# Turning the latent-attention key projection over: one key per partition, then transposed, with ten weight splits moved from GpSimd to VectorE

## The reference, cut to what matters

```python
def mla_expand(c_kv, k_rope, w_kvup, qk_k_norm):
    B, K = c_kv.shape[0], c_kv.shape[1]
    kv = (c_kv @ w_kvup).reshape(B, K, MLA_HEADS, MLA_NOPE_DIM + MLA_V_DIM)
    k_nope, v = kv[..., :MLA_NOPE_DIM], kv[..., MLA_NOPE_DIM:]
    kr = jnp.broadcast_to(k_rope[:, :, None, :], (B, K, MLA_HEADS, MLA_ROPE_DIM))
    k = rmsnorm(jnp.concatenate([k_nope, kr], axis=-1), qk_k_norm)
    return k, v
```

## Time and profile before

| | us |
|---|---|
| median of 3 runs | 1162.91 |
| lowest, highest | 1159.22, 1162.91 |
| profiled execution, its own time | 1165.85 |
| profiled execution, span from first to last instruction | 1164.0 |
| TensorE busy | 1124.8 (97%) |
| VectorE, ScalarE, GpSimd busy | 642.1, 508.1, 353.4 |
| mean granted TensorE clock | 0.976 of full |

### The profile page before, as it was taken

How to read it: one execution, slowest core, us unless ns; L and a number is a source line. 1 busy time by engine, 2 the same in 40 slices (tenths; PEclk the granted TensorE clock), 3 DMA queues, 4 the chain that set the end, 5 groups by cost and what they waited for, 6 DMA issues and landing times.

```text
span 1164.0 us, 21685 instructions
## 1 busy us (share of the span) xinstructions
PE 1124.8 (97%) x7726; PEld 1076.0 (92%) x7726; DVE 642.1 (55%) x1018; ACT 508.1 (44%) x874; POOL 353.4 (30%) x242
## 2 busy tenths in 40 slices
PE   5899999999999999999989999999999999999998
PEld 4798889899999999999978988998999999999998
DVE  5635665444566655653355457654445756665443
ACT  4453534544454444433244434545444544444322
POOL 3566325465112111100027653455531211111000
PEclk9998879999999999999989988999999999999999
DMA  6422222332443544444433232233235444444443
GB/s 207 149 87 98 96 73 91 109 109 93 145 161 114 177 144 152 154 146 153 154 101 110 85 103 91 92 109 100 101 109 163 146 132 165 154 144 146 162 145 118
DMA packets 46823, 148.04 MB, mean 127 GB/s; under 512 B 8185, under 2 KB 11353, under 8 KB 46745
## 3 DMA queue, kind: packets, MB, share of 16 engines
q1 hardware_dynamic: 40472, 144.07, 37.2%
q10 hardware_dynamic: 6272, 2.92, 0.9%
HBM read 143.75 MB, written 3.22 MB: 126 GB/s over the span
## 4 chain that ended last, share of the span: by engine, by line
PE 86%; DVE 5%; issue 4%; DMA 2%; POOL 2%; ACT 1%; SPq 0%; ACTq 0%; DVEq 0%; POOLq 0%
PE psum L407 25%; PE psum L408 24%; PE psum L409 24%; POOL wsum L1567 1%; DMA scratch<-brel 1%; PE psum L466 1%; PE psum L513 1%; PE psum L506 1%; DVE tR L1368 1%; PE psum L518 1%; DVE stdk L1149 1%; PE psum L488 1%; PE psum L651 1%; PE psum L653 1%; PE psum L652 1%
## 5 line engine op out<-in xcount | busy, mean ns | idle before, releaser
L407 PE MATMUL psum<-AH,WH 128*128 128x320 f32 x1344 | 428.6, 319 | 14.2 <-DVE AL L1137 14.2
L408 PE MATMUL psum<-AL,WH 128*128 128x320 f32 x1344 | 419.9, 312 | 0.0
L409 PE MATMUL psum<-AH,WL 128*128 128x320 f32 x1344 | 419.7, 312 | 0.0
L407 PEld LDWEIGHTS psum<-AH,WH 128*128 128x128 f32 x1344 | 256.5, 191 | 27.4 <-DVE AL L1137 18.1
L1523 POOL TENSOR_TENSOR WL<-raw,WH 128x1024 fp32r<-128x1024 f32 x86 | 209.4, 2444 | 231.2 <-ACT WH L805 230.2
L805 ACT CAST WH<-raw 128x1024 fp32r<-128x1024 f32 x178 | 185.2, 1044 | 185.2 <-PE psum L409 169.9
L408 PEld LDWEIGHTS psum<-AL,WH 128*128 128x128 f32 x1344 | 257.0, 191 | 0.8 <-issue 0.2
L409 PEld LDWEIGHTS psum<-AH,WL 128*128 128x128 f32 x1344 | 256.7, 191 | 0.0
L1123 DVE TENSOR_TENSOR WL<-raw,WH 128x1024 fp32r<-128x1024 f32 x90 | 110.0, 1224 | 132.6 <-ACT WH L805 131.7
L1275 DVE TENSOR_TENSOR WL<-raw,WH 128x1024 fp32r<-128x1024 f32 x88 | 107.6, 1223 | 49.3 <-ACT WH L914 48.2
L1528 POOL TENSOR_TENSOR fab<-fa,fb 128x320 f32<-128x320 f32 x44 | 38.7, 880 | 269.6 <-DVE fb L1280 269.6
(11 more groups left out here) (230 smaller groups left out, 1691.7 us busy)
## 6 DMA issues: line engine op xcount, KB each, us to landing
raw<-w_all SPq DMA_DIRECT2D x267, 512.0 KB, 3.3
X<-x_in SPq DMA_DIRECT2D x2, 640.0 KB, 5.1
y_out<-X SPq DMA_DIRECT2D x2, 640.0 KB, 4.1
ckv<-lat_in ACTq DMA_DIRECT2D x2, 512.0 KB, 5.1
lat_out<-ckv ACTq DMA_DIRECT2D x2, 320.0 KB, 2.9
scratch<-brel SPq DMA_DIRECT2D x1, 510.0 KB
cst<-cst_in SPq DMA_DIRECT2D x1, 481.0 KB, 8.8
bias<-scratch SPq DMA_DIRECT2D x8, 48.0 KB, 2.2
```

What stands on the lines that cost most here:

```text
L407: mm(out, WH[:, slot, c0:c0 + cols], high, start=first, stop=False)
L408: mm(out, WH[:, slot, c0:c0 + cols], low, start=False, stop=False)
L409: return mm(out, WL[:, slot, c0:c0 + cols], high, start=False, stop=last)
```

## The change

The K projection is turned over and done like that of V, in seven blocks of 128 keys (`key_rows`): latents stationary, 512 key columns (8 heads by 64) moving, result with one key per partition. The norm is then a sum along the free axis: ScalarE squares (`key_square`), VectorE sums (`tensor_reduce`), ScalarE takes the root of eight numbers a key (`key_root`), VectorE takes the reciprocal and scales the plain columns into `Kn` (`key_scale`), GpSimd scales the rotary columns. TensorE transposes each head back (`turn_keys`, eight transposes a block), and ScalarE and VectorE copy four heads each into `Kt`, with the gain (`key_columns`). The rotary rows are turned once a layer (`turn_rope`). `stat_k`, `turn_k`, `spread_k`, `apply_k`, `square_k` and GpSimd's copies of the rotary rows are gone. The last `turn_keys` stands behind the first of the ten units.

VectorE splits units 12 to 21 (those for which q runs, `U_POOL + q + 1 + LEAD`), which GpSimd did before; GpSimd still splits unit 11, and VectorE waits for that at q = 0. GpSimd clears `qz` later, after that split, since `Kn` and `sqn` share its memory. ScalarE's rounding of unit 7 moves ahead of `ckvH`; units 7 to 9 are split by GpSimd one after the other. The product of the two gains is made inside the layer and no longer before the loop.

```diff
+        def key_rows(l, kb):
+
+            if kb == 0:
+                pe.wait_ge(s.tile_free, l * NT + T_QL + 2)
+            elif kb >= 2:
+                pe.wait_ge(s.kn_ready, l * KB + kb - 1)
+            out = psum[:, kbank(kb), :]
+            for c in range(2):
+                kh, kl = ckvH[:, c, key0(kb):key0(kb) + 128], ckvL[:, c, key0(kb):key0(kb) + 128]
+                wh = WH[:, U_KVK % RING, :].rearrange("k (p c n) -> k c p n", p=4, c=2)[:, c]
+                wl = WL[:, U_KVK % RING, :].rearrange("k (p c n) -> k c p n", p=4, c=2)[:, c]
+                mm(out, kh, wh, start=c == 0, stop=False)
+                mm(out, kl, wh, start=False, stop=False)
+                last = mm(out, kh, wl, start=False, stop=c == 1)
+            last.then_inc(s.kn_full, 1)
...
+        def turn_keys(l, kb):
+
+            pe.wait_ge(s.kn_rope, l * KB + kb + 1)
+            pe.wait_ge(s.kn_ready, l * KB + kb + 1)
+            for h in range(MH):
+                if kb > 0 and h % 4 == 0:
+                    if h == 0:
+                        pe.wait_ge(s.kt_act, l * KB + kb)
+                    else:
+                        pe.wait_ge(s.kt_dve, l * KB + kb)
+                last = nc.tensor.transpose(psum[0:QK, h // 4, (h % 4) * 128:(h % 4) * 128 + 128],
+                                           Kn[:, kb % 2, h, :], ident)
...
+            for kb in range(KB):
+                key_rows(l, kb)
+                value_rows(l, kb)
+                if kb > 0:
+                    turn_keys(l, kb - 1)
 
             for q in range(10):
                 dense(l, U_POOL + q, T_POOL + q)
                 if q == 6:
+                    pe.wait_ge(s.kr_square, l + 1)
                     stat_one(l, N_SWK, s.sq_swk, l + 1, blk, 128, SQ[:, 3, :], T)
-                if q < 6:
-                    stat_k(l, q + 2)
-                if q == 6:
-                    turn_k(l)
-                if q >= 8:
-                    spread_k(l, 2 * q - 16)
-                    spread_k(l, 2 * q - 15)
                 if q == 0:
+                    turn_keys(l, KB - 1)
...
+        def key_square(l, kb):
+
+            act.wait_ge(s.kn_full, l * KB + kb + 1)
+            if kb >= 2:
+                act.wait_ge(s.k_ssq, l * KB + kb - 1)
+            A(sqn[:, kb % 2, :], psum[:, kbank(kb), :], ACT.Square).then_inc(s.k_square, 1)
...
+            for kb in range(KB):
+                key_square(l, kb)
+                value_copy(l, kb)
+                key_root(l, kb)
+                if kb > 0:
+                    key_columns(l, kb - 1)
             high(l, 10)
...
+        def key_scale(l, kb):
+
+            dve.wait_ge(s.k_square, l * KB + kb + 1)
+            v.tensor_reduce(ssq[:, kb, :], sqn[:, kb % 2, :].rearrange("p (h d) -> p h d", h=MH), AX.X, ALU.add) \
+                .then_inc(s.k_ssq, 1)
+
+            dve.wait_ge(s.k_std, l * KB + kb + 1)
+            v.reciprocal(rk[:, kb, :], rk[:, kb, :]).then_inc(s.k_recip, 1)
+            dve.wait_ge(s.k_recip, l * KB + kb + 1)
+            TT(Kn[:, kb % 2, :, 0:NOPE], psum[:, kbank(kb), :].rearrange("p (h d) -> p h d", h=MH),
+               rk[:, kb, :, None].to_broadcast([128, MH, NOPE]), ALU.mult).then_inc(s.kn_ready, 1)
...
+                if q == 0:
+                    key_columns(l, KB - 1)
+                    dve.wait_ge(s.split_ready, l * NU + U_POOL + LEAD + 1)
+                low(l, U_POOL + q + 1 + LEAD)
...
-                apply_k(l, 8 + h)
...
+            for kb in range(KB):
+
+                if kb >= 2:
+                    pool.wait_ge(s.kt_full, 2 * (l * KB + kb) - 2)
+                pool.wait_ge(s.k_recip, l * KB + kb + 1)
+                g_.tensor_tensor(Kn[:, kb % 2, :, NOPE:QK], krn[:, kb:kb + 1, :].to_broadcast([128, MH, ROPE]),
+                                 rk[:, kb, :, None].to_broadcast([128, MH, ROPE]), ALU.mult).then_inc(s.kn_rope, 1)
+            low(l, U_KVV + 3)
+            pool.wait_ge(s.kt_full, 2 * (l * KB + KB))
+            low(l, U_POOL + LEAD)
+            g_.memset(qz[:], 0.0).then_inc(s.qz_zero, 1)
```

More of the change, by code:

```diff
@@ L37 @@
 KB = -(-NKEY // 128)
-KPART = ((0, 3), (3, KB))
 POOLS = (2, 4, 8, 16)
@@ L456, in stat_mix @@
             mm(psum[:, b, 0:T], ones, ssum[:], start=True, stop=True).then_inc(s.stat_full, 1)
-        def stat_k(l, h):
-            if h == 0:
-                pe.wait_ge(s.std_ready, l * NSTAT + 2)
-            for part, (b0, b1) in enumerate(KPART):
-                pe.wait_ge(s.sq_k, l * 16 + 2 * h + part + 1)
-                for b in range(b0, b1):
-                    n = min(128, NKEY - b * 128)
-                    last = mm(psum[0:n, 0, b * MH + h:b * MH + h + 1], sqf[0:QK, b * 128:b * 128 + n], ones[0:QK, 0:1],
-                              start=True, stop=True)
-                last.then_inc(s.k_stat, 1)
@@ L470, in turn_k, with turn_rope @@
[L470 to L490 removed]
+        def turn_rope(l):
+            for kb in range(KB):
+                last = nc.tensor.transpose(psum[:, 3, kb * ROPE:(kb + 1) * ROPE],
+                                           krT[64:96, key0(kb):key0(kb) + 128], ident[64:96, 64:96])
+            last.then_inc(s.kr_turned, 1)
@@ new lines, in value_rows @@
+        def value_rows(l, kb):
+            if kb == 0:
+                pe.wait_ge(s.split_ready, l * NU + U_KVV + 1)
+                pe.wait_ge(s.tile_free, l * NT + T_QL + 3)
+            elif kb >= 2:
+                pe.wait_ge(s.v_ready, l * KB + kb - 1)
+            out = psum[:, kbank(kb) + 1, :]
+            for c in range(2):
+                kh, kl = ckvH[:, c, key0(kb):key0(kb) + 128], ckvL[:, c, key0(kb):key0(kb) + 128]
+                wh = WH[:, U_KVV % RING, c * 512:c * 512 + 512]
+                wl = WL[:, U_KVV % RING, c * 512:c * 512 + 512]
+                mm(out, kh, wh, start=c == 0, stop=False)
+                mm(out, kl, wh, start=False, stop=False)
+                last = mm(out, kh, wl, start=False, stop=c == 1)
+            last.then_inc(s.v_full, 1)
@@ L718, in _ @@
                 last.then_inc(s.tile_full, 1)
-                spread_k(l, 8 + h)
             for g in range(2):
@@ L954, in _ @@
             root(l, N_KV, 128, T, 256)
+            high(l, 7)
             act.wait_ge(s.stat_applied, l * NNORM + N_KV + 1)
@@ L1296, in _ @@
         dve.wait_ge(s.par_in, 16)
-        for e in range(DEPTH):
-            TT(kgain[0:QK, e:e + 1], par[0:QK, e * NPAR + C_GK:e * NPAR + C_GK + 1],
-               par[0:QK, e * NPAR + C_GQ:e * NPAR + C_GQ + 1], ALU.mult).then_inc(s.gains, 1)
-        dve.wait_ge(s.gains, DEPTH)
         with dve.Fori(0, DEPTH) as l:
@@ L1333, in _ @@
             scaled(l, T_QL + 2, qlr[:, 2, :])
[L1334 to L1338 removed]
+            rope_mean(l)
+            for kb in range(KB):
+                key_scale(l, kb)
+                if kb > 0:
+                    key_columns(l, kb - 1)
             for q in range(10):
@@ L1407, in _ @@
                         .then_inc(s.tile_free, 1)
-            for e in range(4, 8):
-                apply_k(l, e)
             dve.wait_ge(s.swq_root, l + 1)
@@ L1571, in _ @@
                     .then_inc(s.win_ready, 1)
-            for u in range(U_PW, gate_unit(BR_GATES)):
+            pool.wait_ge(s.split_ready, l * NU + U_PW + LEAD + 1)
+            for u in range(U_PW + 1, gate_unit(BR_GATES)):
                 low(l, u + LEAD)
```

232 lines of the change are left out of this document (87 added, 145 removed).

## The result

| | before | after |
|---|---|---|
| median of 4 runs each, us | 1162.82 | 1129.83 |
| lowest, highest | 1159.22, 1162.91 | 1127.06, 1131.10 |
| ratio, 95% interval | | 0.9734 [0.9695, 0.9774] |
| profiled execution: own time, span | 1165.85, 1164.0 | 1130.26, 1128.4 |
| TensorE, VectorE, ScalarE, GpSimd busy | 1124.8, 642.1, 508.1, 353.4 | 1081.7, 653.5, 503.6, 293.5 |

The change takes 33.0 us off the median and 35.6 off the span of the profiled execution. A second timing of the changed kernel gave 1127.87 and 0.9723 [0.9696, 0.9750]. The kernel before had medians of 1159.8 to 1159.9 in the three later timings, so its profiled execution (1165.85) was about 6 us slower than usual. Its times there went from 1155.6, at a granted clock of 0.985, to 1169.1, at 0.971.

The account below looks back on a forecast made before the run. TensorE, busy 97% of the span, was taken as the bound. Terms 8.0 - 17.4 - 3.1 - 16.8 + 1.0 = -28.3 took 1165.85 to 1137.5, less 2.9 for the median: forecast 1134, range 1126 to 1142 (8 in 10: 1119 to 1149).

Parts of the forecast that it names:

- A: TensorE's stretch of key and value blocks, 22.4 us before: 26.4 after, 4.0 more in each layer.
- The 3.3 us chain: Key norm over several engines, from value copy to scaled keys: 3.3 us, hidden behind 5.2 us of TensorE work.
- The 5.9 us at the high end: The key norm's length at 1024-element prices for each 512: about 5.9 us, costing 10 us over 14 blocks.
- B: TensorE's stretch from keys and values to the window-key sum: 33.6 us in place of 42.3, 8.7 less per layer.
- The three rounds: GpSimd's adds and VectorE's work between the first and fourth difference before the window-key sum: 5.2, 5.2 and 5.8 us.
- C: TensorE's stretch from window-key sum to pooling weights: 19.2 us in each layer, 1.8 and 1.3 less.
- D: TensorE's stretch from pooling weights to first scores: 27.5 us in each layer, 11.5 and 5.3 less.
- The start: Layer beginnings: 0.5 us less from earlier remainders, 1.5 more if GpSimd's unit 7 split gets in first; net +1.0.
- TensorE-bound: Rival: chain before the window-key sum hidden and clock stays up, 18.8 us less, 1115; chance 0.12.
- That the clock takes a part back: Rival: slow clock lasts into gates and heads, or window rounds take longer; 8 to 15 us higher, about 1146; chance 0.24.
- The two slower ones: Rivals in key blocks: norm's chain sets the pace, 1180, chance 0.04; transposes lower TensorE's clock, 1186, chance 0.04.
- That nothing comes of it: Rival: new norm costs TensorE what the old did and moved splits bring nothing, 1163; chance 0.02.

Follow-up runs that it names:

- the last two experiments: Changed kernel with each key block's scaling made three times, 1134.52 us; changed kernel with each key-block transposition made four times, 1162.57 us.
- the first two: Changed kernel with ten splits back on GpSimd, 1138.71 us; kernel before with only those ten splits given to VectorE, 1153.62 us.
- three such edits: Changed kernel with units 8 and 9 split later by GpSimd, and units 22 to 24 and 11 split by VectorE: 1118.33 us together.
- the three kernels with waits of over a microsecond: Changed kernel with window-key sum two units later, 1125.70 us; with window-key squares earlier, 1125.50; with those squares and three split edits, 1118.04.

## Why the prediction was right, point by point

**The direction and the mechanism** held: TensorE's list lost the key sums, the spreads and `apply_k`'s waits, and no rival took their place. The forecast of 1134 was 4.2 us above the median. That it came so close is in part luck: the four stretches took 37.9 us off where 29.3 was predicted, and 2.6 us lost elsewhere, which the prediction had at nothing, made up for some of it. The -35.6 is also measured from an execution of the kernel before that was slower than usual.

**A** (+4.0) was +4.2 and +4.5. The transposes were cheaper than charged (0.80 a set, not 0.88) and the first wait longer (1.52 and 1.80, not 0.8). It was due to an operation so small that the prediction did not count it at all, `krm`. The 3.3 us chain was right: the third key block ends at 56.72, its scaled keys are there at 60.06, and its transposes begin at 61.81, so nothing waits. The sum over 512 took 0.69, the scaling 0.69. (The 5.9 us at the high end cannot be added up from the prices that stand beside it: 1.43 + 1.04 + 0.3 + 0.2 + 2.44 make 5.4. Nothing hangs on it.)

**B** (-8.7) was -9.9. The end of the chain was as described, with the wait of 5.1 for the 6 predicted, released by the square of `kT`. The three rounds took 4.9, 4.6 and 5.6 us (starts of the differences, 88.33, 93.24, 97.87 and 103.48) where 5.2, 5.2 and 5.8 were taken, and the first difference came at 14.7 instead of 15.3. The prediction had the squares behind the fourth difference and its rounding as a matter of course; they need neither, and stood there by their place in ScalarE's queue alone.

**C** (-1.8, -1.3) was -4.6 and -2.7. The step that failed is "I charge 3.5 for the slow units now in C": the 72 matmuls of the last three units took 11.80 and 13.20 us, where at 0.151 they take 10.87. The clock cost 0.9 and 2.3, not 3.5. What was removed came to 6.1 and 5.7, not 5.4: the last of the four groups of spreads took 1.68 and 1.23 us, not 0.95, part of it at the lower clock. The sums of the window queries with their waits cost 0.7 more, for the 0.6 predicted. So 20.97 - 6.1 + 0.9 + 0.7 = 16.5 against 16.4, and 20.51 - 5.7 + 2.3 + 0.7 = 17.8 against 17.8.

**D** (-11.5, -5.3) was -10.6 and -9.0. The 27.5 us taken for each layer was the mis-sized term. In layer two the 0.93 window of the earlier trace rows begins behind the pooling weights, and the 21 matmuls before the first spread stood at 281 ns each (3.37 + 2.53 us; 3.7 in the changed kernel): 2.2 us of slow clock that were never counted. In layer one 28.4 is one of the lengths that D takes, and it goes with a slow clock at its beginning. That there would be "no long idle time in the query heads" was wrong there: 2.09 us, where 0.3 had been left for new waits. Both layers together were put at 55.0 and took 52.3. Of layer one's -10.6 some 6 us are the lower clock of the profile before (39.0 there, 32.8 in layer two with the same work).

**The start** (+1.0) was -0.3. Its mechanism, GpSimd getting in first, is real: it happened in two other profiles, and made TensorE wait 2.78 and 2.90 us there. It did not in this one.

**The rivals.** TensorE-bound: it would have needed the chain hidden, and with the squares moved ahead B is indeed 27.4, but the time falls by 2.4 and not by 18.8, since the chain is then waited for elsewhere. That the clock takes a part back: it did, by 0.9 and 2.3 us in C and with a granted clock of 0.88 in D of layer one, which is less than the 12 us that this rival asked for. The two slower ones are refuted by the last two experiments. One argument against the first of them did fail: not all of VectorE's operations with a single input ran at their usual length beside GpSimd's, as `krm` shows with 2.09 us in place of 0.17. That nothing comes of it is refuted by the first two.

## What to carry to other kernels

When a chain over several engines ends in a wait, look at each queue for what stands ahead of the last step without being needed by it; but take such a wait's length as the most that can be gained, since here 5.06 us gave 1.2 to 2.8. Where VectorE and GpSimd both read SBUF, place the long operations of one against stretches in which the other has none, or give them to one engine: three such edits gave 9.5 us. Turning a result so that the reduced axis is the free one cost TensorE a fixed price per block (0.8 us for eight transposes) and saved it all sums and spreads of the factors.

## What the runs showed of the hardware

- An operation of VectorE on 128x7 elements, with one SBUF input, took 2.09 us beside GpSimd's splits and 0.17 without.
- Which of VectorE and GpSimd gets in first is decided by tenths of a microsecond: 0.41 us ahead, the remainder took 1.23; 0.12 behind, 3.37.
- With 54% of TensorE's time in transposes of fp32 blocks the granted clock was 1.00; one transposition of 128 keys by 96 elements took 0.10 to 0.11 us among others.
- What the lower clock costs behind a wait varies within one run: behind the same 5.06 us the 72 matmuls took 11.80 us in layer one and 13.20 in layer two. The twelve pooling matmuls took 3.29 to 3.37 us in the three kernels with waits of over a microsecond ahead of the window queries' sums, and anything from 2.26 to 3.24 where that wait is 0.5; what decides that was not found. The stretch behind them went with it: 23.9 us at 2.26, 28.4 from 2.99 on, in seven profiles.
